# Two blocks in float32 on one core: the second block's gated FFNs take most of their first products from a scaled x, its high and low part in one matmul of 512 columns

## What is computed

```python
def swiglu_ffn(x, g, w_in, w_out):
    h = rms_norm(x, g)                          # x * rsqrt(mean(x^2) + 1e-6) * g
    gate, up = jnp.split(h @ w_in, 2, axis=-1)  # w_in: 1024 x 5632
    return (jax.nn.silu(gate) * up) @ w_out     # w_out: 2816 x 1024

x = x + 0.5 * swiglu_ffn(x, ffn1_norm[layer], ffn1_w_in[layer], ffn1_w_out[layer])
```

## Time and profile before

| | |
|---|---|
| three runs | 2184.45, 2185.46, 2187.73 us |
| the profiled execution, its own time | 2187.13 us |
| its span in the trace | 2185.3 us |
| PE matmul busy | 2164.1 us (99%), 17084 matmuls |
| DVE, ACT, POOL busy | 1519.5 (70%), 1194.3 (55%), 296.3 us (14%) |
| transfers | 356.56 MB, mean 163 GB/s |

### The profile page before, as it was taken

The page is one execution under the profiler, slowest core; times in us unless marked ns, Lnnn a source line. Parts: engine busy times, 40 slices in busy tenths (PEclk is TensorE's granted clock), DMA queues, the critical chain, the costliest instruction groups (busy, mean ns, idle before and its releaser), DMA issues.

```text
span 2185.3 us, 42508 instructions
## 1 busy us (share of the span) xinstructions
PE 2164.1 (99%) x17084; PEld 2061.6 (94%) x17084; DVE 1519.5 (70%) x2635; ACT 1194.3 (55%) x2060; POOL 296.3 (14%) x273
## 2 busy tenths in 40 slices
PE   8999999999999999999999999999999999999999
PEld 8899989999999999999999999999999998989998
DVE  6767686887578677779856666676666666886664
ACT  5655465665446554566655544455445444665453
POOL 1000112000100011210002210002210220232211
PEclk9999999999999999999999999999999999999999
DMA  7335436356744354455565655345555555435554
GB/s 259 116 126 143 135 109 197 116 175 176 218 117 126 115 152 137 131 173 164 184 201 193 194 186 180 127 134 179 188 184 177 194 187 185 154 117 172 185 184 135
DMA packets 97381, 356.56 MB, mean 163 GB/s; under 512 B 10929, under 2 KB 11057, under 8 KB 97057
## 3 DMA queue, kind: packets, MB, share of 16 engines
q1 hardware_dynamic: 94752, 342.47, 49.6%
q0 software_dynamic: 2000, 10.38, 1.8%
q10 hardware_dynamic: 432, 0.99, 0.1%
HBM read 352.68 MB, written 1.12 MB: 162 GB/s over the span
## 4 chain that ended last, share of the span: by engine, by line
PE 92%; DVE 5%; ACT 2%; issue 1%; DMA 1%; DVEq 0%; ACTq 0%; SPq 0%
PE pd L1389 24%; PE pd L1400 23%; PE pd L1397 23%; PE pd L1382 6%; PE pd L1385 3%; DVE wlo L2315 2%; PE pt L1558 1%; PE ps L1389 1%; PE pd L1574 1%; PE ps L1397 1%; PE ps L1400 1%; PE ps L1533 1%; PE ps L1767 1%; PE pd L1680 1%; ACT whi L1871 1%
## 5 line engine op out<-in xcount | busy, mean ns | idle before, releaser
L1871 ACT ACTIVATE whi<-raw 128x1024 fp32r<-128x1024 f32 x618 | 651.1, 1055 | 592.4 <-PE pd L1400 498.5
L1389 PE MATMUL pd<-x,whi 128*128 128x256 f32 (+2 forms) x3328 | 973.1, 292 | 1.6 <-DVE tb L2840 1.1
L2315 DVE TENSOR_TENSOR wlo<-raw,whi 128x1024 fp32r<-128x1024 f32 x618 | 767.6, 1243 | 256.6 <-ACT whi L1871 255.6
L1400 PE MATMUL pd<-x,wlo 128*128 128x256 f32 (+2 forms) x3319 | 941.9, 284 | 0.5 <-DVE wlo L2315 0.4
L1397 PE MATMUL pd<-x,whi 128*128 128x256 f32 (+2 forms) x3319 | 941.3, 284 | 0.0
L1389 PEld LDWEIGHTS pd<-x,whi 128*128 128x128 f32 x3328 | 627.8, 189 | 27.1 <-issue 21.0
L1400 PEld LDWEIGHTS pd<-x,wlo 128*128 128x128 f32 x3319 | 626.4, 189 | 0.9 <-DVE wlo L2315 0.9
L1397 PEld LDWEIGHTS pd<-x,whi 128*128 128x128 f32 x3319 | 624.7, 188 | 2.4
L1382 PE MATMUL pd<-a,whi 128*128 128x512 f32 x528 | 184.9, 395 | 0.0
L3103 POOL TENSOR_TENSOR acc<-acc,sq 128x256 f32<-128x256 f32 (+2 forms) x78 | 74.0, 949 | 808.9 <-ACT sq L1930 807.4
L3113 POOL TENSOR_TENSOR tb<-tb,rs 128x256 f32<-128x256 f32 x88 | 122.0, 1386 | 375.3 <-ACT tb L2173 375.3
(11 more groups left out here) (391 smaller groups left out, 3322.8 us busy)
## 6 DMA issues: line engine op xcount, KB each, us to landing
raw<-in_w SPq DMA_DIRECT2D x648, 512.0 KB, 3.6
TA<-scr POOLq DMA_DIRECT2D x2, 1392.0 KB, 11.5
C<-in_c POOLq DMA_DIRECT2D x1, 2432.0 KB, 10.7
TD<-scr POOLq DMA_DIRECT2D x2, 1056.0 KB, 8.3
TD<-scr POOLq DMA_DIRECT2D x2, 768.0 KB, 13.2
h<-in_h SPq DMA_DIRECT2D x4, 272.0 KB, 5.7
out<-result SPq DMA_DIRECT2D x4, 256.0 KB, 2.5
C<-in_c POOLq DMA_DIRECT2D x1, 800.0 KB, 14.6
```

Source lines behind the costliest of these rows:

```text
L1389: e.matmul(out, hi, xh, start=begin, stop=False)
L1400: self.block_done(e.matmul(out, lo, xh, start=False, stop=end), c, j)
L1871: e.activation(m.whi[i][:, 0:n], m.raw[c % NRAW][:, 0:n], ACT.Copy).then_inc(*self.up("ac_hi", ("hi", c)))
L2315: e.tensor_tensor(m.wlo[i][:, 0:n], m.raw[c % NRAW][:, 0:n], m.whi[i][:, 0:n].bitcast(F32), ALU.subtract).then_inc(*self.up("dv_lo", ("lo" ...
```

## The change

In each gated FFN of the second block, the tiles `up` from the tenth on (from the thirteenth in stage 4) are wide and read a scaled x, z, kept split in y2, the place of the mixers' output y, now one tensor of [128, 2, 8, 256]. The tiles ahead stay as they were: the first three (six in stage 4), and six more (`NARROW_UP`). Eight slices are made by `scaled_x`, a slice every half chunk from the root on, with `z_hi` always on ACT. The wide pairs use `up_add` (DVE) and `up_mul` (POOL), which were in the code; `silu_in` of a wide tile adds the halves of its bank with a `tensor_reduce` (`both`) and does not multiply by rs. The waits for a place to be free (`x_unused`, `y_unused`) are adapted.

```diff
--- before.py
+++ after.py
@@ -27,6 +27,7 @@
 NRAW, NSPL, LEAD = 4, 3, 2
 NMORE, EARLY = 4, 8.0
 WIDE_DOWN = 6
+NARROW_UP = 6
 SBUF_BEGIN, SBUF_END = 16576, 229376
 GROUPS = [(0, 16), (16, 128), (144, 128)]
 CHUNKS = [(0, 16), (16, 64), (80, 64), (144, 64), (208, 64)]
@@ -686,19 +687,24 @@
         self.boundaries.append((int(self.now()), []))
         self.post_norm(stage, self.now())
 
-    def scaled_x(self, stage, r0):
+    def scaled_x(self, stage, r0, every=0.1):
 
         for k in range(8):
-            self.step("dv", r0 + 0.05 + 0.1 * k, "z_norm", stage, k)
-            self.step(*(("ac", r0 + 0.1 + 0.1 * k) if k else ("dv", r0 + 0.04)), "z_hi", stage, k)
-            self.step("dv", r0 + 0.17 + 0.1 * k, "z_lo", stage, k)
+            r = r0 + every * k
+            self.step("dv", r + 0.05, "z_norm", stage, k)
+            self.step(*(("ac", r + 0.1) if k or stage > 3 else ("dv", r + 0.04)), "z_hi", stage, k)
+            self.step("dv", r + 0.17, "z_lo", stage, k)
 
     def swiglu(self, which, l, stage):
         c0 = self.flush()
         up = self.tiles(stage, "up", f"{which}_in{l}", 0, 2 * NFF, 8, T2)
         pairs = [(up[j], up[NFF + j]) for j in range(NFF)]
         order, n = [t for p in pairs for t in p], 6 if stage == 4 else 3
-        self.await_root(self.dense(order[:n], True, 3))
+        first = order[:n]
+        for t in order[n + NARROW_UP:]:
+            t.x, t.wide = "w", True
+        self.await_root(self.dense(first, True, 3))
+        r0 = self.root_at
         self.dense(order[n:])
         self.flush()
         down = self.tiles(stage, "down", f"{which}_out{l}", 0, 8, NFF, T2, "a")
@@ -724,6 +730,7 @@
                 self.step("dv", s + 0.15, "silu_up", stage, j, v)
             self.step("ac", s + 0.5 + late, "act_hi", stage, j)
             self.step("dv", s + 0.8 + late, "act_lo", stage, j)
+        self.scaled_x(stage, r0 + 0.2, 0.5)
         if stage == 4:
             self.step("gp", c0 + 8, "load_c2", c0 + LEAD + NMORE - 1)
         self.step("ac", d0 + 1.5, "table")
@@ -1103,7 +1110,8 @@
         self.C2 = sb("C2", [128, n2])
         for n in ("wb", "wc", "wd"):
             self.ring[n] = [sb(f"{n}{i}", [128, 384]) for i in range(RINGS[n])]
-        self.yh, self.yl = sb("yh", [128, 8, T2], F32R), sb("yl", [128, 8, T2], F32R)
+        self.y2 = sb("y2", [128, 2, 8, T2], F32R)
+        self.yh, self.yl = self.y2[:, 0], self.y2[:, 1]
         self.ring["su"] = [sb(f"su{i}", [128, 16]) for i in range(4)]
         self.top = arena
         self.RQ, self.RK, self.RG = (sb(n, [128, 4, T2]) for n in ("RQ", "RK", "RG"))
@@ -1309,7 +1317,19 @@
 
 def x_unused(plan, stage):
 
-    return [] if stage == 0 else [("used", plan.final[stage - 1, "x"]), ("used", plan.final.get((stage - 1, "z"), 0))]
+    return [] if stage == 0 else [("used", plan.final[stage - 1, "z" if STAGES[stage - 1][0] == "conv_ffn" else "x"])]
+
+
+def y_unused(plan, stage):
+
+    return [("used", plan.final[stage - 1, kind]) for kind in ("y", "w") if (stage - 1, kind) in plan.final]
+
+
+def scaled_place(m, plan, stage, k):
+
+    if stage > 3:
+        return m.yh, m.yl, y_unused(plan, stage)
+    return m.xh, m.xl, [("early", stage, k)]
 
 
 def conv_place(engine, stage, t):
@@ -1355,8 +1375,9 @@
         l = STAGES[stage][1]
         if tile.x == "x":
             return m.xh[:, k, at], m.xl[:, k, at], ("x_hi", stage, k), ("x_lo", stage, k)
-        if tile.x == "z":
-            return m.xh[:, k, at], m.xl[:, k, at], ("z_hi", stage, k), ("z_lo", stage, k)
+        if tile.x in ("z", "w"):
+            xh, xl, _ = scaled_place(m, self.p, stage, k)
+            return xh[:, k, at], xl[:, k, at], ("z_hi", stage, k), ("z_lo", stage, k)
         if tile.x == "m":
             return m.mh[:, k, at], m.ml[:, k, at], ("m_hi", l, k), ("m_lo", l, k)
         if tile.x == "o":
@@ -1376,7 +1397,7 @@
         hi, lo = (w[self.p.split_buf[c]][:, j * 128:(j + 1) * 128] for w in (m.whi, m.wlo))
         xh, xl, high, low = self.moving(tile, k)
         if tile.wide:
-            part = m.a2 if tile.x == "a" else m.x2
+            part = m.a2 if tile.x == "a" else m.y2
             for s in self.ahead(("hi", c), high, low, self.free("pd", tile.key) if begin else None):
                 e.wait_ge(*s)
             e.matmul(self.buf("pd", tile.key), hi, part[:, :, k, tile.span], start=begin, stop=False)
@@ -1918,9 +1939,10 @@
     def z_hi(self, stage, k):
 
         e, m, (_, at) = self.e, self.m, entering(stage)
-        for s in self.ahead(("z", stage, k), ("early", stage, k)):
-            e.wait_ge(*s)
-        e.activation(m.xh[:, k, at], m.u8[:, k, at], ACT.Copy).then_inc(*self.up("ac_norm", ("z_hi", stage, k)))
+        xh, _, room = scaled_place(m, self.p, stage, k)
+        for s in self.ahead(("z", stage, k), *room):
+            e.wait_ge(*s)
+        e.activation(xh[:, k, at], m.u8[:, k, at], ACT.Copy).then_inc(*self.up("ac_norm", ("z_hi", stage, k)))
 
     def squares(self, name, stage, k, src, at, ready):
         e = self.e
@@ -2226,7 +2248,7 @@
     def y_hi(self, stage, k, scale):
         e, m = self.e, self.m
         src, ready = mixed_place(m, stage, k)
-        for s in self.ahead(*ready):
+        for s in self.ahead(*ready, *y_unused(self.p, stage)):
             e.wait_ge(*s)
         e.activation(m.yh[:, k, :], src, ACT.Copy, scale=scale).then_inc(*self.up("ac_split", ("y_hi", stage, k)))
 
@@ -2344,9 +2366,10 @@
 
     def z_lo(self, stage, k):
         e, m, (_, at) = self.e, self.m, entering(stage)
-        for s in self.ahead(("z", stage, k), ("z_hi", stage, k)):
-            e.wait_ge(*s)
-        e.tensor_tensor(m.xl[:, k, at], m.u8[:, k, at], m.xh[:, k, at].bitcast(F32), ALU.subtract).then_inc(
+        xh, xl, room = scaled_place(m, self.p, stage, k)
+        for s in self.ahead(("z", stage, k), ("z_hi", stage, k), *room):
+            e.wait_ge(*s)
+        e.tensor_tensor(xl[:, k, at], m.u8[:, k, at], xh[:, k, at].bitcast(F32), ALU.subtract).then_inc(
             *self.up("dv_norm", ("z_lo", stage, k)))
 
     def normed(self, dst, src, stage, at, scale=1.0):
@@ -3003,7 +3026,7 @@
     def y_lo(self, stage, k, scale):
         e, m = self.e, self.m
         src, _ = mixed_place(m, stage, k)
-        for s in self.ahead(("y_hi", stage, k)):
+        for s in self.ahead(("y_hi", stage, k), *y_unused(self.p, stage)):
             e.wait_ge(*s)
         hi = m.yh[:, k, :].bitcast(F32)
         if scale == 1.0:
```

## The result

The changed kernel takes 2208.68 us, the median of five runs (2206.86 to 2211.03), beside 2185.73 for the kernel before: a ratio of 1.0101, with a 95% interval of 1.0088 to 1.0113. The forecast was 2200.0 (2191 to 2207) and the range 2190 to 2209, so it is slower, as forecast, but above the forecast's own band and 0.3 us inside the range. The profiled execution's span is 2206.9 us, 21.6 more than before. One time in all that follows, 2321.88 us of best2_288 at a granted clock of 0.85, is of a slower state of the chip and is left out of that kernel's median.

A forecast was written before the change was run, and what follows sets the result against it. PE, busy 99% of the span, was taken to bound the kernel. A 5.4 us gain against waits of 5.0 + 2 x 5.8 + 3.5 gave +14.7 us on the median, rounded 2200.0 us; range 2190 to 2209.

The forecast's parts named there:

- the forecast's own band: Whole kernel: a time of 2191 to 2207 us, given a chance of 0.76.
- the clock rival: Gated FFNs: a wait drops the clock to half, one to three times per stage, giving 2207 to 2220 us; chance 0.05.
- PE's gain: First products of four gated FFNs: 1096 blocks made wide, each saving 0.0049 us by one matmul fewer, 5.4 us.
- Stage 7's waits: PE waits for `lo` of C0+5, C0+6 and C0+7: 2.15, 1.24 and 1.59 us, together 5.0 us.
- The walk: Stage 7 behind the root: DVE's and ACT's steps timed in list order, `lo` of C0+5 ending at 14.88 (1680 subtracted).
- stages 6 and 9: First wait 0.79 us longer than stage 7's: 2.94 + 1.24 + 1.59 = 5.8 us in each.
- Stage 4's waits: PE waits for `lo` of C0+9, C0+10 and C0+11: 0.34, 1.56 and 1.57 us, together 3.5 us.
- The sum: Whole kernel: gain of 5.4 us against waits of 5.0, twice 5.8 and 3.5 us, +14.7 us in all.
- The reduction: Wide pairs on DVE: 512 PSUM columns to 256 taken at 0.69 us, bounds 0.41 and 1.00, hidden from PE.
- The backlog-hidden rival: Narrow chunks behind the root: DVE's backlog never reaches PE, only the gain is left, 2180.1 us; chance 0.09.
- the one with a single late `lo`: Gated FFNs: only each stage's first late `lo` costs, 8.4 us less the 5.4 gain, 2188.5 us; chance 0.07.
- a sign of being wrong: First-product stretches: `lo` of C0+5 under 1 us behind before's, a low clock, or PE waiting in wide chunks.

The follow-up runs named there:

- best2_288: The change with y2 rows 1152 bytes apart, z_lo 0.7 chunk behind its slot, slices every 0.85 chunk (stage 4: 1.0, two more narrow tiles): 2191.44 us.
- z_only: The change with the slices z made but read by no tile, all first products staying narrow: 2209.88 us, ratio 1.0110 to the kernel before.
- pad: The change with y2's rows 272 elements (1088 bytes) apart instead of 256 (1024 bytes): 2204.83 us, ratio 1.0085 to the kernel before.
- wide_only: The change with wide tiles reading unscaled x, no slices made, residual factor 1e-5 (output not the reference's): 2179.43 us, ratio 0.9970 to the kernel before.
- slow: The change with a slice every 0.75 chunk instead of 0.5: 2194.83 us, ratio 1.0036 to the kernel before.
- best2_256: As best2_288, but with y2's rows 256 elements (1024 bytes) apart, as in the change: 2191.33 us, ratio 1.0021 to the kernel before.
- lag: The change with z_lo of each slice due 0.7 chunk behind its slot instead of 0.17, behind the next z_norm: 2195.48 us, ratio 1.0045 to the kernel before.

## Why the prediction was right, and what it mis-sized

The mechanism was as told: DVE and ACT had some 35% and 49% of these stretches free and still made PE wait, since the slices stand ahead of `lo` in strict lists. z_only shows that they alone make the loss. That the time fell inside the range is in part luck: it lies above the forecast's own band (2191 to 2207), and the range reached to 2209 for the clock rival's sake, which is not what made the difference. The two errors were the waits, 3.8 us too small, and PE's gain, 3.6 us too large. Step by step:

- **Stage 7's waits**: forecast 2.15, 1.24 and 1.59, 5.0 us; measured 5.6 (in z_only, without a low clock, 2.4, 1.4 and 1.9). The walk's times came within 0.1 us up to `lo` of C0+5. The error is the start of z_lo behind z_hi: 0.10 us each time, where the hop from DVE to ACT had given 0.03 for both ways. Eight slices of the difference are 0.6 us a stage. The same accounts for most of stages 6 and 9: 6.5 measured, 5.8 forecast. It is not the price of every hop from ACT to DVE, for `lo` keeps its 0.03 behind `hi`; z_lo also waits for z_norm, a step of its own engine, but no run tests whether that is the cause.
- **Stage 4's waits**: forecast 3.5 us, measured 5.3. The step that failed is the reading of the earlier trace rows: its row at 1190.84 is the third block of C0+9, not its first. Counted back from down's start, 280 blocks of 0.3549 us ahead of 1289.53, the chunk begins at 1190.16, and a matmul of line 1389 starts at 1190.13. So PE wanted `lo` 0.7 us earlier than was written. Of the other 1.1 us z_lo's later start makes 0.6 (eight slices); where the rest lies in the walk stays open.
- **PE's gain**: forecast 5.4 us at 0.0049 a block, measured 1096 x 0.0016 = 1.8. This is the largest single error, 3.6 us, and pad gives it back (0.3500 us a block). Down's wide tiles were the wrong neighbour to price from, for their operand lies otherwise in memory, which the declarations show. The Trainium skill's 2.5 ns per matmul (TensorE: Matmul & The Clock Gate, "Wait — 56ns, not 53.3ns?") is what none of the traces shows: one matmul fewer saved 1.6 ns in the change, 3.2 where a block took 0.3517 us, 4.9 in pad, 5.7 in wide_only and 8.2 in stage 9 of slow.
- **The sum**: waits 23.9 instead of 20.1 and gain 1.8 instead of 5.4, so +22.1 against the forecast +14.7. The stretches are 22.2 us longer, the span 21.6.
- **The reduction** was taken at 0.69 us and took 0.692 (0.692 x 137 = 94.8 us), hidden as said: PE had no idle time in wide tiles. The warning of the Trainium skill against `tensor_reduce` on a hot path (VectorE: DVE Perf Modes, "Rules for kernel authors") is borne out in the length, 0.692 us where silu_in took 0.41, but it cost no time here, while DVE had a fifth of each wide chunk free.
- **The backlog-hidden rival and the one with a single late `lo`** fall: in z_only three `lo` were late in each stage. wide_only, at 2179.43, is what the first would have looked like (forecast 2180.1).
- **The clock rival**: the time lies in its band (2207 to 2220) and the clock did fall in three of the four stages, which was named as a sign of being wrong; but z_only is as late in every stage without any fall. See the last section.

## What to carry to other kernels

In engines with strict lists, free time on average says nothing: walk the two lists against each other over the few chunks in which new steps stand, take the hop between two engines from the same pair of steps, not from another, and check each chunk's start by counting blocks back from a mark that is sure. Slices moved by a tenth of a chunk, one of them across another step, decided 1.0 to 1.8 us of PE's first wait a stage here, because ACT's table load stood behind it. And price a matmul from one whose operand lies the same way in memory.

## What the runs showed that was not expected

**The clock fell around the waits, with a price only where no other wait followed.** In the change's profiled execution the granted clock was 0.5 (1.2 GHz) for 6.8 us from 1511.9 in stage 6, 0.8 us before the end of a wait of 3.0 us; for 3.4 us from 1706.5 in stage 7, 1.0 us behind a wait of 2.1; and for 3.4 us from 2023.9 in stage 9, 0.2 us behind a wait of 3.0. The stretches, with the columns of the earlier trace rows:

```profile
1512.10:1518.90 6.80, 6.17 (x29) 6.17 (x30) 5.14 (x12) 3.34 (x6) 0.00 (x0) 0.51 0.33 117
...
1706.60:1710.00 3.40, 3.40 (x18) 3.40 (x18) 2.85 (x7) 1.36 (x3) 0.00 (x0) 0.51 0.40 143
...
2023.90:2027.30 3.40, 3.40 (x18) 3.40 (x18) 2.29 (x6) 2.09 (x4) 0.00 (x0) 0.51 0.44 154
```

In z_only, with waits as long, it stayed at full in all four stages; in pad it fell in stages 6 and 9, again without a difference by C0+8. In stage 6 the change's PE was 5.4 us late at C0+6 against z_only's 3.3, but 6.6 and 6.5 at C0+8: the slow matmuls only filled time in which PE would have waited for DVE. In lag, where they stood behind the only long wait, they cost some 0.65 us a stage.

**Where the moving operand lies shows in a matmul's pace.** With rows of 1024 bytes a wide block took 0.3533 us in all four stages of the change, alternating 0.346 and 0.361 from one block to the next, but 0.3467 in stage 9 of slow and in two stages of best2_256; at 1056 to 1152 bytes it took 0.3500 to 0.3517. x2 gave 0.3492, though its layout (rows of 1088 bytes, parts 8704 bytes apart) is pad's, which gave 0.3500; down's a2 gave 0.350 in every stage of every kernel. So the spacing alone does not set it, and one kernel can have two values in two stages. Within a stage it keeps one. What sets which one, and why, stays open: nothing here tried it.
